# Three small edits: a square moved behind the residual, eight bias additions moved from ScalarE to VectorE, an activation table loaded earlier

## The chip, the cores and the metric

The kernel runs on one core of a Trainium2 chip. The metric is the time of one execution on the device in microseconds (us); the median of three executions of the kernel before is 2815.58 us, the lowest 2815.47 and the highest 2816.88.

TensorE is called PE in the profile, ScalarE ACT, VectorE DVE, GpSimd POOL, and SyncE SP.

## The reference

Two transformer stacks run one after the other on 256 tokens of width 1024, in fp32.

The first stack puts 16 meta tokens in front (272 rows) and has two layers. A layer is: a SwiGLU feed-forward and a layer norm; a mixer (short convolution and latent attention with gates) and a layer norm; a second feed-forward and a layer norm. In the latent attention the query latents (256 columns) and the key-value latents (128 columns) are each normalized by their root mean square before they are projected again:

```python
q = (rms_norm(c_q, q_norm_g) @ w_uq).reshape(...)
kv = (rms_norm(c_kv, kv_norm_g) @ w_ukv).reshape(...)
```

The second stack has two layers. Both start with an rms norm and a token mixer with three branches. The first layer then has a dense SwiGLU and the second a mixture of 8 experts (top 2 of a router, `swiglu` of width 3584 for each). A last rms norm closes the kernel:

```python
h = layer_norm(ALPHA * h + 0.5 * swiglu(h, ...), ln_g[l, 2], ln_b[l, 2])   # end of the first stack
...
h = rmsnorm(x, norm_g)                                                     # start of the second
...
gate = softmax(top_v); out = silu(xb @ w_gate[e]) * (xb @ w_up[e]) @ w_down[e]
```

## The kernel before, in words

Each engine has a program of its own, written out in full by hand; semaphores are the only link between them, and an engine runs its program strictly in order. Activations lie transposed: 8 chunks of 128 channels on the partitions, 272 or 256 tokens along the free dimension. Every fp32 product is made of three fp16 matmuls, high times high, high times low and low times high (`parts`, L2081 to L2085). Weights come in units of 2048 columns through four slots. For each unit SP starts the loads, ACT makes the high half (`split`, L705), DVE the low half (L1260), PE multiplies, and ACT or DVE takes the sums out of PSUM. PE may start a unit when its low half is there (`parts_ready`) and when the PSUM banks that it writes have been emptied (`act_evac`, `vec_evac`).

Three places matter here.

**Place A, the latents, in the loop over the six units of `win` (L900 to L919), once in each of the first stack's two layers.** ACT's program at step u=2 is: the square of the three latent chunks into `tmp` (L904); `residual` (L796 to L800), eight biased copies that turn the scaled rows `sq` into the residual `h`; the split of a later unit (L705); and the emptying of unit 2 (L898). PE, when it has finished unit 2, waits for `lat_squared` (L2334), sums the squares (L2335 to L2337), places the rotary key (L2340), and goes on with unit 3. ACT takes the square roots at step u=3 (L913, L914), DVE inverts them and scales the latents (L1461, L1464), and PE waits for the two halves of the result (`lat_ready`, L2344) after unit 5.

**Place B, the last layer norm of the first stack (`layer_norm` with `last=True`).** DVE scales chunk after chunk: `t(c)` (L1386) makes `sq[c]`, `u(c+1)` (L1376) centers the next chunk, and a drain ends the step. ACT follows each chunk with two operations: the square of `sq[c]` plus the bias (L788), which PE sums for the rms norm behind it (L2285), and the same sum unsquared, the residual `h[c]` (L789). After the eighth chunk PE runs its filler matmuls (`keep_warm`, L2237), ACT takes the root (L828) and DVE the reciprocal (L1404).

**Place C, the router of the second stack's second layer.** PE makes the router's logits and transposes the tokens into PSUM (L2698, two halves); DVE finds the two best experts. ACT's program here is: the exponential of the difference of the two (L1187); the high halves of the two token halves out of PSUM (L1190, `xt_hi_ready`); and then a one-element Silu (L1191) before which the table with Silu is loaded. DVE makes the low half of each token half behind ACT (`rows_low`, L1776), between the two the ranks (L1780) and the marks of the first expert (L1787). PE gathers the first expert's rows with them (L2742), ACT empties the gathered rows (L1199, L1231), and PE starts on the first expert's weights (L2083). The eight experts follow one another in the same program, with six slots of weights.

Of the kernel before, what the change touches and what calls it, by code (L numbers as in the profile page):

```python
# [39 lines left out]
META = 16  # L40
# [654 lines left out]
def act_program(act, k, i, out):  # L695
# [80 lines left out]
    def layer_norm(n, b0, q, following, last=False):  # L776

        act.wait_ge(k.ln_rest, n + 1)
        t = kept(n)
        act.activation(k.tmp[:, 1, t], k.ps[:, 4, t], ACT.Square).then_inc(k.rest_squared, 1)  # L780
        act.wait_ge(k.ln_spread, n + 1)
        act.activation(k.std[:, 0, t], k.tmp[:, 1, t], ACT.Sqrt, bias=k.eps[:, 0:1]).then_inc(k.ln_std, 1)
        split(following + 2, q, UNIT)
        if last:

            for c in range(KC):
                act.wait_ge(k.ln_scaled, n * KC + (c + 1))
                act.activation(k.sq2[:, c, :], k.sq[:, c, META:T1], ACT.Square, bias=k.col[:, b0 + c:b0 + c + 1]).then_inc(k.rms_squared, 1)  # L788
                act.activation(k.h[:, c, META:T1], k.sq[:, c, META:T1], ACT.Identity, bias=k.col[:, b0 + c:b0 + c + 1])  # L789
            return  # L790

        for c in range(KC):
            act.wait_ge(k.ln_scaled, n * KC + (c + 1))
            act.activation(k.x_hi[:, c, t], k.sq[:, c, t], ACT.Identity, bias=k.col[:, b0 + c:b0 + c + 1]).then_inc(k.x_hi_ready, 1)
# [80 lines left out]
    for l in range(DEPTH):  # L875
# [23 lines left out]
        win, mid, side = S1["win"], S1["mid"], S1["side"]  # L899
        for u in range(win.units):  # L900
            late = u + AHEAD - win.units
            if u == LAT_SQUARED:
                act.drain()
                act.activation(k.tmp[:, :, :], k.mix1[:, 12:15, :], ACT.Square).then_inc(k.lat_squared, 1)  # L904
            if u == 2:
                residual(C1["ln_b"], ALL1)
            if u >= 1:
                split(win.first + u + AHEAD, q, win.size if late < 0 else win.after[late])

            if u == LAT_ROOT:  # L910
                act.wait_ge(k.lat_mean, l + 1)
                act.drain()
                act.activation(k.std[:, 0, :], k.ps[:, 4, 0:T1], ACT.Sqrt, bias=k.eps[:, 1:2], scale=float(D) / 256)  # L913
                act.activation(k.std[:, 1, :], k.ps[:, 5, 0:T1], ACT.Sqrt, bias=k.eps[:, 1:2], scale=float(D) / 128).then_inc(k.lat_std, 1)  # L914
            if u == LAT_HI:
# [269 lines left out]
        expert_split(u, 0)  # L1185
    act.wait_ge(k.lg_ready, 1)
    act.activation(k.rt[:, :, 1], k.rt[:, :, 0], ACT.Exp).then_inc(k.lg_exped, 1)  # L1187
    for t in range(2):
        act.wait_ge(k.xt_turned, t + 1)
        act.activation(k.xt_hi[:, t, :], k.ps[:, 2 * t:2 * t + 2, :].rearrange("p b n -> p (b n)"), ACT.Copy).then_inc(k.xt_hi_ready, 1)  # L1190
    act.activation(k.warm[:, :], k.eps[:, 0:1], ACT.Silu)  # L1191

    def gathered(bank):
        return k.ps[:, bank:bank + 2, :].rearrange("p b (c s) -> p (b c) s", s=P)
# [60 lines left out]
def vec_program(vec, k, i, out):  # L1255
# [114 lines left out]
    def layer_norm(n, g0, b0, last=False):  # L1370
# [19 lines left out]

        def lo(c):
            return vec.scalar_tensor_tensor(k.x_lo[:, c, cols], k.sq[:, c, cols], k.col[:, b0 + c:b0 + c + 1], k.x_hi[:, c, cols], ALU.add, ALU.subtract)
        for c in range(KC + 1):
            if last:

                if c < KC:
                    t(c)
            else:
                scaled(c, t, lo, (n + 1) * KC)
            vec.drain()  # L1400
# [679 lines left out]
def pe_program(pe, k, i, out):  # L2080
# [240 lines left out]
    for l in range(DEPTH):  # L2321
# [8 lines left out]
        def towards_latents(u):  # L2330
# [1 line left out]
                return  # L2332

            pe.wait_ge(k.lat_squared, l + 1)  # L2334
            pe.matmul(k.ps[:, 4, 0:T1], k.mean_w[:, :], k.tmp[:, 0, :], start=True, stop=False)  # L2335
            pe.matmul(k.ps[:, 4, 0:T1], k.mean_w[:, :], k.tmp[:, 1, :], start=False, stop=True)
            pe.matmul(k.ps[:, 5, 0:T1], k.mean_w[:, :], k.tmp[:, 2, :], start=True, stop=True).then_inc(k.lat_mean, 1)  # L2337

            for n in range(2):
                a = pe.matmul(k.ps[0:QK, 6 + n, 0:T1], k.place[:, n, :], k.mix1[0:ROPE, 15, :], start=True, stop=True)  # L2340
# [584 lines left out]
```

## Time and profile before

| | before |
|---|---|
| median of 3 executions | 2815.58 us |
| the profiled execution | 2815.58 us |
| its span, first to last instruction | 2813.8 us |
| what lies around the span | 1.8 us |
| mean granted clock of TensorE | 0.992 |
| PE busy | 2750.0 us (98%) |
| DVE busy | 1981.1 us (70%) |
| ACT busy | 1612.1 us (57%) |
| POOL busy | 700.7 us (25%) |

The profiled execution took the median's time, so its span can be used with no correction. A busy PE includes matmuls that overlap in its pipeline, so 98% does not say that there is nothing to gain; what counts at each place is which wait ends last there. In a timeline the columns are the start, the duration, the engine, the source line, the operation and its tiles, how many, and in brackets how long the engine stood idle before it and what released it.

### The profile page before, as it was taken

What the parts mean: (1) busy time and instruction counts of PE and PEld (TensorE: products, weight loads), DVE (VectorE), ACT (ScalarE), POOL (GpSimd) and SP (SyncE); (2) the same over time, 40 slices, a digit from 0 to 9 for tenths busy, and PEclk for the clock granted to TensorE, in tenths of its full rate; (3) what the DMA queues carried; (4) which work ended last, traced back from release to release, by engine and by line L of the source; (5) the groups of instructions that cost most, each with busy time, mean ns of one, the idle gap of its engine ahead of it and who ended that gap; (6) DMA issues with size and microseconds to landing.
All of it is one profiled execution on the core that took longest, in us unless ns stands there. A gap on an engine that the chain in (4) does not pass through costs nothing.

```text
span 2813.8 us, 68029 instructions
## 1 busy us (share of the span) xinstructions
PE 2750.0 (98%) x28028; PEld 2294.9 (82%) x28028; DVE 1981.1 (70%) x1906; ACT 1612.1 (57%) x1731; POOL 700.7 (25%) x562
## 2 busy tenths in 40 slices
PE   9999999999999999999999999999999999999998
PEld 8887778888877888887788897888879788797794
DVE  4567575465575755666755566779899898998986
ACT  5445653353356544555544455656777776777765
POOL 4315022121122221120122002144234243242331
PEclk9999999999999999999999999999999999999999
DMA  9764367576643676553666663469999999999995
GB/s 240 172 198 130 92 181 201 164 192 175 188 138 109 177 209 174 162 187 109 179 182 171 205 196 125 150 229 369 377 394 380 386 388 377 394 382 384 389 378 228
DMA packets 657516, 665.64 MB, mean 237 GB/s; under 512 B 25302, under 2 KB 513116, under 8 KB 657276
## 3 DMA queue, kind: packets, MB, share of 16 engines
q1 hardware_dynamic: 655696, 659.75, 71.3%
q8 instruction: 189, 3.10, 0.5%
q0 software_dynamic: 704, 0.59, 0.4%
q10 hardware_dynamic: 876, 1.79, 0.2%
q14 instruction: 51, 0.42, 0.0%
HBM read 661.01 MB, written 1.05 MB: 235 GB/s over the span
## 4 chain that ended last, share of the span: by engine, by line
PE 90%; DVE 4%; ACT 2%; issue 2%; DVEq 2%; POOLq 0%; POOL 0%; ACTq 0%
PE ps L2083 23%; PE ps L2085 23%; PE ps L2084 23%; PE ps L2809 3%; PE ps L2808 3%; PE ps L2807 3%; PE ps L2124 1%; PE ps L2130 1%; PE ps L2125 1%; DVE w_lo L1260 1%; PE ps L2412 1%; PE ps L2432 1%; DVE sq L1386 1%; PE ps L2500 1%; PE ps L2502 1%
## 5 line engine op out<-in xcount | busy, mean ns | idle before, releaser
L2083 PE MATMUL ps<-x_hi,w_hi 128*128 128x128 f16 (+2 forms) x5440 | 1231.1, 250 | 15.1 <-DVE prod L1275 5.4
L2085 PE MATMUL ps<-x_hi,w_lo 128*128 128x128 f16 (+2 forms) x5440 | 1230.5, 250 | 0.0
L2084 PE MATMUL ps<-x_lo,w_hi 128*128 128x128 f16 (+2 forms) x5440 | 1230.5, 250 | 0.0
L1260 DVE SCALAR_TENSOR_TENSOR w_lo<-w,w_hi 128x2048 f16<-128x2048 f32 (+4 forms) x338 | 692.7, 2060 | 303.3 <-ACT w_hi L705 301.4
L705 ACT ACTIVATE w_hi<-w 128x2048 f16<-128x2048 f32 (+4 forms) x338 | 560.9, 1669 | 94.8 <-PE ps L2085 70.5
L2083 PEld LDWEIGHTS ps<-x_hi,w_hi 128*128 128x128 f16 x5440 | 534.3, 98 | 70.4 <-issue 14.4
L2084 PEld LDWEIGHTS ps<-x_lo,w_hi 128*128 128x128 f16 x5440 | 534.2, 98 | 46.1
L2085 PEld LDWEIGHTS ps<-x_hi,w_lo 128*128 128x128 f16 x5440 | 534.1, 98 | 42.9
L1753 DVE SCALAR_TENSOR_TENSOR w_lo<-w,w_hi 128x2048 f16<-128x2048 f32 x224 | 534.3, 2411 | 40.6 <-ACT w_hi L1180 40.4
L1180 ACT ACTIVATE w_hi<-w 128x2048 f16<-128x2048 f32 x224 | 416.9, 1901 | 28.6 <-DMA w<-in_moe_w_gate 11.6
L2065 POOL CAST ff<-pb 128x512 f16<-128x512 f32 x56 | 135.5, 2419 | 568.2 <-DVE pb L1845 568.2
L2083 PE MATMUL ps<-ff,w_hi 128*128 128x272 f16 (+1 forms) x880 | 243.4, 277 | 0.0
L2084 PE MATMUL ps<-ff,w_hi 128*128 128x272 f16 (+1 forms) x880 | 243.4, 277 | 0.0
L2085 PE MATMUL ps<-ff,w_lo 128*128 128x272 f16 (+1 forms) x880 | 243.4, 277 | 0.0
L1180 ACT ACTIVATE ff<-mix 128x2048 f16<-128x2048 f32 x112 | 211.5, 1903 | 16.9 <-DMA mix<-in_moe_w_down 15.3
L718 ACT ACTIVATE tmp<-ps 128x272 f32<-128x272 f32 (+1 forms) x110 | 43.0, 391 | 299.9 <-PE ps L2085 297.1
L2083 PE MATMUL ps<-x_hi,ff 128*128 128x128 f16 x1024 | 173.2, 219 | 0.0
L2084 PE MATMUL ps<-x_lo,ff 128*128 128x128 f16 x1024 | 173.2, 219 | 0.0
L2067 POOL TENSOR_TENSOR ff<-pb,ff 128x512 f16<-128x512 f32 x56 | 167.6, 2993 | 8.1 <-issue 0.2
L1902 POOL CAST ff<-prod 128x272 f32 (+3 forms) x110 | 57.6, 524 | 442.0 <-DVE prod L1275 441.5
L1275 DVE SCALAR_TENSOR_TENSOR prod<-tmp,ps 128x272 f32<-128x272 f32 (+1 forms) x110 | 47.4, 431 | 133.8 <-ACT tmp L718 123.9
L1753 DVE SCALAR_TENSOR_TENSOR mix<-mix,ff 128x2048 f16<-128x2048 f32 x56 | 130.9, 2337 | 14.7 <-ACT ff L1180 14.7
(390 smaller groups left out, 4307.5 us busy)
## 6 DMA issues: line engine op xcount, KB each, us to landing
w<-in_ffn_w_up SPq DMA_DIRECT2D x176, 512.0 KB, 5.0
w<-in_moe_w_gate SPq DMA_DIRECT2D x80, 1024.0 KB, 8.4
w<-in_moe_w_up SPq DMA_DIRECT2D x80, 1024.0 KB, 8.6
w<-in_moe_w_down SPq DMA_DIRECT2D x64, 1024.0 KB, 7.7
w<-in_w_in SPq DMA_DIRECT2D x112, 512.0 KB, 4.6
mix<-in_moe_w_down SPq DMA_DIRECT2D x48, 1024.0 KB, 8.1
w<-in_mix_w_in SPq DMA_DIRECT2D x64, 512.0 KB, 5.0
mix<-in_moe_w_gate SPq DMA_DIRECT2D x32, 1024.0 KB, 8.9
```

Of the source, the lines that this page charges most:

```text
L705: act.activation(k.w_hi[:, s, 0:size], k.w32[:, s, 0:size], ACT.Copy, scale=WS).then_inc(k.hi_ready, 1)
L1180: act.activation(k.e_hi[s], k.e_w32[s], ACT.Copy, scale=WS).then_inc(k.hi_ready, 1)
L1260: vec.scalar_tensor_tensor(k.w_lo[:, s, 0:size], k.w32[:, s, 0:size], WS, k.w_hi[:, s, 0:size], ALU.mult, ALU.subtract).then_inc(k.parts_r ...
L1753: vec.scalar_tensor_tensor(k.e_lo[s], k.e_w32[s], WS, k.e_hi[s], ALU.mult, ALU.subtract).then_inc(k.parts_ready, 1)
L2065: pool.tensor_copy(k.a_hi3[:, rows, :], prod)
L2067: pool.tensor_tensor(k.a_lo3[:, rows, :], prod, k.a_hi3[:, rows, :], ALU.subtract).then_inc(k.ff_ready, 1)
L2083: pe.matmul(acc, w_hi, x_hi, start=first, stop=False)
L2084: pe.matmul(acc, w_hi, x_lo, start=False, stop=False)
L2085: return pe.matmul(acc, w_lo, x_hi, start=False, stop=last)
L2807: pe.matmul(acc, k.a_hi3[:, ff, :], k.e_hi[s][:, w], start=ff == 0, stop=False)
L2808: pe.matmul(acc, k.a_lo3[:, ff, :], k.e_hi[s][:, w], start=False, stop=False)
L2809: a = pe.matmul(acc, k.a_hi3[:, ff, :], k.e_lo[s][:, w], start=False, stop=ff == EC - 1)
```

## The change

Three edits, in ACT's, DVE's and PE's programs. The arithmetic is the same.

1. Place A: at step u=2 the square of the latents goes from the front of the step to behind the residual and the split, just ahead of the emptying of unit 2. Its result goes to `sq[0:3]` instead of `tmp`, since the residual has by then read `sq`, and PE reads it there. The drain ahead of the roots at u=3 goes.
2. Place B: ACT's eight additions of the bias into `h` go (L789). DVE does them as `plain(c)`, one step behind the scaling: chunk c-1 in step c, behind `t(c)` and `u(c+1)` and ahead of the drain.
3. Place C: the one-element Silu, and so the load of its table, goes from behind the two copies of the tokens to directly behind the exponential.

```diff
@@ layer_norm, ACT @@
                 act.activation(k.sq2[:, c, :], k.sq[:, c, META:T1], ACT.Square, bias=...).then_inc(k.rms_squared, 1)
-                act.activation(k.h[:, c, META:T1], k.sq[:, c, META:T1], ACT.Identity, bias=...)
@@ the loop over win, ACT @@
-            if u == LAT_SQUARED:
-                act.drain()
-                act.activation(k.tmp[:, :, :], k.mix1[:, 12:15, :], ACT.Square).then_inc(k.lat_squared, 1)
             if u == 2:
                 residual(C1["ln_b"], ALL1)
             if u >= 1:
                 split(win.first + u + AHEAD, q, win.size if late < 0 else win.after[late])
+            if u == LAT_SQUARED:
+                act.drain()
+                act.activation(k.sq[:, 0:3, :], k.mix1[:, 12:15, :], ACT.Square).then_inc(k.lat_squared, 1)
             if u == LAT_ROOT:
                 act.wait_ge(k.lat_mean, l + 1)
-                act.drain()
                 act.activation(k.std[:, 0, :], k.ps[:, 4, 0:T1], ACT.Sqrt, ...)
@@ before the experts, ACT @@
     act.activation(k.rt[:, :, 1], k.rt[:, :, 0], ACT.Exp).then_inc(k.lg_exped, 1)
+    act.activation(k.warm[:, :], k.eps[:, 0:1], ACT.Silu)
     for t in range(2):
         act.wait_ge(k.xt_turned, t + 1)
         act.activation(k.xt_hi[:, t, :], ..., ACT.Copy).then_inc(k.xt_hi_ready, 1)
-    act.activation(k.warm[:, :], k.eps[:, 0:1], ACT.Silu)
@@ layer_norm, DVE @@
+        def plain(c):
+            vec.tensor_scalar(k.h[:, c, META:T1], k.sq[:, c, META:T1], k.col[:, b0 + c:b0 + c + 1], None, ALU.add)
         for c in range(KC + 1):
             if last:
                 if c < KC:
                     t(c)
+                if c > 0:
+                    plain(c - 1)
@@ towards_latents, PE: the three matmuls of L2335 to L2337 read k.sq[:, 0..2, :] instead of k.tmp[:, 0..2, :] @@
```

## Rows read from the trace of the kernel before

**Rows 1.** The page, part 4: the chain that ended last, by engine.

```profile
PE 90%; DVE 4%; ACT 2%; issue 2%; DVEq 2%; POOLq 0%; POOL 0%; ACTq 0%
```

**Rows 2.** Timeline of ACT in the experts: the emptying that ends each expert.

```profile
2108.68 1.11 ACT L1219 ACTIVATE mix<-ps,gate_now 128x1024 f16<-128x1024 f32 x1 [5.13 <-PE ps L2809]
...
2338.30 1.11 ACT L1219 ACTIVATE mix<-ps,gate_now 128x1024 f16<-128x1024 f32 x1 [4.38 <-PE ps L2809]
```

**Rows 3.** Timeline of ACT at place A, layer 0.

```profile
220.37 0.62 ACT L898 ACTIVATE mix<-ps 128x544 f32<-128x544 f32 x1
221.07 0.88 ACT L904 ACTIVATE tmp<-mix 128x816 f32<-128x816 f32 x1
221.87 3.39 ACT L799 ACTIVATE h<-sq,col 128x272 f32<-128x272 f32 x8
225.16 1.89 ACT L705 ACTIVATE w_hi<-w 128x2048 f16<-128x2048 f32 x1
226.96 0.60 ACT L898 ACTIVATE mix<-ps 128x544 f32<-128x544 f32 x1
```

**Rows 4.** Timeline of PE at place A, layer 0.

```profile
224.76 0.62 PE L2335 MATMUL ps<-tmp,mean_w 128*128 128x272 f32 x2
```

**Rows 5.** The square's line: count, duration in ns, first and last start.

```profile
L904 ACT ACTIVATE tmp<-mix x2: 883/884/884, 221.1 to 800.4; 128x816 f32<-128x816 f32 x2
```

**Rows 6.** Timeline of DVE: the latents' low half, for which PE waits after unit 5.

```profile
241.65 1.00 DVE L1476 TENSOR_TENSOR y_lo<-sq,y_hi 128x816 f16<-128x816 f32 x1
```

**Rows 7.** The chain that ended last, behind unit 5: start, duration, what.

```profile
244.06 0.13 PE ps L2085
...
244.73 1.90 ACT w_hi L705
```

**Rows 8.** Timeline at place B, one step of DVE and ACT behind it.

```profile
1155.90 0.48 DVE L1386 SCALAR_TENSOR_TENSOR sq<-h,col,rstd 128x256 f32<-128x256 f32 x1
1156.31 0.41 DVE L1376 TENSOR_TENSOR h<-h,ps 128x256 f32<-128x256 f32 x1
1156.42 0.51 ACT L788 ACTIVATE ff<-sq,col 128x256 f32<-128x256 f32 x1 [0.59 <-DVE sq L1386]
1156.80 0.48 DVE L1386 SCALAR_TENSOR_TENSOR sq<-h,col,rstd 128x256 f32<-128x256 f32 x1
...
1164.54 1.75 DVE L1404 RECIPROCAL rstd<-tmp 128x256 f32<-128x256 f32 x1 [1.91 <-ACT tmp L828]
```

**Rows 9.** Timeline of DVE: a tensor_scalar of 256 columns, then a drain.

```profile
1193.23 0.35 DVE L1561 TENSOR_SCALAR ff<-mix,col 128x256 f32<-128x256 f32 x1
1193.67 1.61 DVE L1564 SCALAR_TENSOR_TENSOR ff<-mix,col,ff 128x255 f32<-128x255 f32 x3
```

**Rows 10.** Timeline at place C.

```profile
1865.12 0.21 ACT L1187 ACTIVATE rt<-rt 128x2 f32<-128x2 f32 x1 [1.35 <-DVE rt L1765]
1865.23 1.00 ACT L1190 ACTIVATE mix<-ps 128x1024 f16<-128x1024 f32 x1
...
1866.27 1.23 DVE L1776 TENSOR_TENSOR mix<-ps,mix 128x1024 f16<-128x1024 f32 x1
...
1867.55 1.28 ACT L1191 ACT_TABLE_LOAD   x1
...
1868.84 0.20 ACT L1191 ACTIVATE warm<-eps 128x1 f32<-128x1 f32 x1
...
1869.43 1.02 ACT L1199 ACTIVATE x_hi<-ps 128x1024 f16<-128x1024 f32 x1 [0.39 <-PE ps L2742]
...
1872.34 0.26 PE L2083 MATMUL ps<-x_hi,w_hi 128*128 128x128 f16 x1 [1.20 <-ACT x_lo L1231]
```

**Rows 11.** Busy time by stretch (us; PE, PEld, DVE, ACT, POOL), granted clock, DMA share, GB/s.

```profile
1157.00:1164.00 7.00, 5.65 (x19) 2.79 (x20) 5.18 (x13) 6.61 (x16) 0.00 (x0) 1.00 0.01 2
...
1864.00:1872.30 8.30, 5.95 (x50) 5.15 (x48) 7.82 (x23) 5.78 (x8) 4.54 (x4) 0.71 0.39 128
1872.30:1880.00 7.70, 7.66 (x102) 7.69 (x103) 7.23 (x12) 3.52 (x3) 7.70 (x5) 0.72 0.81 278
```

More of the change, by code:

```diff
@@ L788, in layer_norm @@
                 act.activation(k.sq2[:, c, :], k.sq[:, c, META:T1], ACT.Square, bias=k.col[:, b0 + c:b0 + c + 1]).then_inc(k.rms_squared, 1)
-                act.activation(k.h[:, c, META:T1], k.sq[:, c, META:T1], ACT.Identity, bias=k.col[:, b0 + c:b0 + c + 1])
             return
@@ L2334, in towards_latents @@
             pe.wait_ge(k.lat_squared, l + 1)
-            pe.matmul(k.ps[:, 4, 0:T1], k.mean_w[:, :], k.tmp[:, 0, :], start=True, stop=False)
-            pe.matmul(k.ps[:, 4, 0:T1], k.mean_w[:, :], k.tmp[:, 1, :], start=False, stop=True)
-            pe.matmul(k.ps[:, 5, 0:T1], k.mean_w[:, :], k.tmp[:, 2, :], start=True, stop=True).then_inc(k.lat_mean, 1)
+            pe.matmul(k.ps[:, 4, 0:T1], k.mean_w[:, :], k.sq[:, 0, :], start=True, stop=False)
+            pe.matmul(k.ps[:, 4, 0:T1], k.mean_w[:, :], k.sq[:, 1, :], start=False, stop=True)
+            pe.matmul(k.ps[:, 5, 0:T1], k.mean_w[:, :], k.sq[:, 2, :], start=True, stop=True).then_inc(k.lat_mean, 1)
             for n in range(2):
```

## The prediction, made before the changed kernel was built or run

> **What bounds the kernel now.** I read the page first, its chain that ended last. TensorE holds 90% of it, DVE 4% and ACT 2% [rows 1]. So a change on another engine moves the time only where PE stands waiting for it, and the thing to look up at each place is who waits last. The second view is the timeline of the experts, which fill the last third. One ACT operation ends each expert; from its start at 2108.68 to that two experts later, 2338.30, there are 229.62 us, 114.81 for each, and PE releases it each time [rows 2]. A delay ahead of the experts therefore has nothing in them that could give it back. The other views are the timelines of the three edited places, where the reader should compare the end of one engine's operation with the start of the next engine's.
>
> **Place A, the square behind residual and split.** Before, ACT empties unit 1 (220.37 to 220.99), squares from 221.07 to 221.95, runs the eight residual copies from 221.87, the split from 225.16, and empties unit 2 from 226.96 [rows 3]. PE takes up the squares at 224.76, right behind unit 2, with no idle time before it [rows 4]. So the squares lie ready 2.81 us early, and PE pays nothing for them. After the edit the chain on ACT is: an operation that follows undrained starts 0.08 before its predecessor ends (221.87 against 221.95), so the residual starts at 220.99 - 0.08 = 220.91; the split follows 225.16 - 221.87 = 3.29 later, at 224.20, and lasts 1.89, to 226.09; the drain costs the 0.08 seen between 220.99 and 221.07, so the square runs from 226.17 to 227.05; the hand-over to the next engine costs 0.04, as between DVE's end at 1156.38 and ACT's start at 1156.42 [rows 8]. PE begins at 227.09 in place of 224.76: a stall of 2.33 us. The second layer has the same square at 800.4 [rows 5], so twice, 4.66 us.
>
> What is queued behind the late square: only the emptying of unit 2, and since the step's operations are the same ones in another order, it keeps its time of about 226.96. PE needs it for unit 4, over 5 us later. The split comes a microsecond earlier, but PE has not been waiting for it. The roots at step u=3 need PE's three sums. At 0.62 each [rows 4] these end at 227.09 + 3 x 0.62 = 228.95 at the latest; ACT gets to the roots at about 226.96 + 0.60 + 1.89 = 229.45 [rows 3], so they are not delayed, and the drain taken away ahead of them (0.08) lies in cover.
>
> Who gives the stall back? PE's next waits for others. The latents' low half ends at 242.65 [rows 6], while PE finishes unit 5 at 244.19, later anyway. Behind it the chain goes over ACT's split at 244.73 [rows 7], but in ACT's program that split stands behind the emptying of unit 5, so it starts from PE's own end and moves with it. I find no clock of another engine that would absorb the stall, and cost it in full: 4.66 us. Bounds: nothing, if a later wait absorbs it, and 4.66.
>
> **Place B, the bias additions on DVE.** DVE sets the pace: a step is t (0.48 us, next start 0.41 later) and u (0.41), and the next t starts 0.90 after the first [rows 8]. ACT's two operations fit into the same 0.90: its square starts 0.04 after DVE's scaling ends and never falls behind. Removing one of the two from ACT therefore gains nothing, least of all at the end: the last pair is followed by PE's sum and the root, which waits for PE.
>
> The added operation is a tensor_scalar of 128x256 in fp32 out of SBUF. The same form takes 0.35 us, and with a drain behind it the next operation starts 0.44 later [rows 9]. In a step it slips between u and the drain: t to u 0.41, u to plain 0.41 - 0.07 = 0.34 (0.07 being the overlap of t and u, 1156.38 - 1156.31), plain and drain 0.44. A step is 1.19 in place of 0.90, so 0.29 more. Steps 1 to 6 with plain(0) to plain(5) lie ahead of the last scaling: 6 x 0.29 = 1.74 us. plain(6) and plain(7) come behind it and hide: DVE sits idle for 1.91 us ahead of the reciprocal [rows 8], and the two need 2 x 0.44, about 0.9. Without that cover they would cost 0.9 more. Bounds: nothing, if ACT's additions had been what held the pace, and 8 x 0.44 = 3.5. I take 1.74, for the nearest row is the same operation of the same size.
>
> Here the trace and the skill differ. The row has 0.35 us for the tensor_scalar. The Trainium skill, page "VectorE: DVE Perf Modes", section "The TRN2 errata — SBUF-src ops pay a fixed extra latency per instruction", tables a VectorE operation out of SBUF at 58 cycles plus half the elements in a doubled mode, which for 256 elements is an estimate of 0.19 us; by it the step would grow by 0.13 and place B would cost 0.8. The row decides.
>
> **Place C, the table loaded before the copies.** Before, ACT takes the exponential at 1865.12, the first copy from 1865.23 to 1866.23, and DVE starts the low half at 1866.27, 0.04 later: it is gated by the copy. Load (1.28) and Silu (0.20) come at 1867.55, and are over at 1869.04, before ACT's next task at 1869.43, for which PE releases it [rows 10]. They cost nothing there. After the edit the load starts right behind the exponential, at about 1865.36, ends at 1866.64, and the Silu is over at 1866.85; the first copy starts 0.09 before that, 1866.76, and ends at 1867.76. DVE's low half starts at 1867.80, 1.53 later than before. Behind it on DVE wait the ranks and the first expert's marks, behind those PE's gather, ACT's emptying of it (1869.43), and PE's first expert matmul at 1872.34 [rows 10]: one chain, each link started by the one before, so 1.53 us later at its end. The second copy ends about 1868.7, before anything asks for it.
>
> The granted clock bears on this term. Its mean is 0.71 from 1864 to 1872.3, where PE is busy for 5.95 of 8.3 us, and 0.72 in the 7.7 us from the first expert matmul on [rows 11]. With the two levels 0.5 (1.2 GHz) and 1 (2.4 GHz) a mean of 0.72 is 7.7 x 0.28 / 0.5 = 4.3 us at the lower one. If the clock returns at the same moment, a later start wastes less: of the 1.53 us half comes back, 0.77 net. If the return moves with the work, all 1.53 stay. I take the middle, 1.15. Bounds: 1.53 - 2.15 = -0.6, if the first expert loses nothing to the clock, and 1.53 + 2.15 = 3.7, if it loses twice as much.
>
> The Trainium skill, page "ScalarE: Activation LUTs", section "What ACT_TABLE_LOAD costs", adds a drain of about 1.38 us to each load. No such gap stands in the trace, where the Silu follows the load at 1868.84, 0.01 after its end; by the page, place C would come out at an estimated 2.5 in place of 1.15.
>
> **Sum.** 4.66 + 1.74 + 1.15 = 7.55 us. The profiled execution took 2815.58, which is the median as well, so 2823.1 us, 0.27% more. About 0.2%, 5.6 us here, is what a measurement of this kernel can tell from no change.
>
> **The rivals.**
> *Absorbed at place A (not slower by a measurable amount).* PE would have waited behind unit 5 in any case, for the latents or for a load, and gives the two stalls back there. Price: 4.66 off, leaving 2.9, 2818.5 us. For it: PE's end at 244.19 is followed by ACT's split on the chain, so PE truly waits there. Against: that wait starts from PE's own unit [rows 7], and the latents are 1.5 us early [rows 6, 7]. It decides as soon as 1.9 of the 7.55 come back, less than one layer's stall.
> *The clock falls where it held.* At place B PE is busy 5.65 of 7 us and the clock holds at 1.00 [rows 11]; with steps a third longer PE thins out, and at place A it stands for 2.33 us. At place C the clock did fall once PE stood. A low stretch as long as the one at place C, 4.3 us, costs half of that, 2.15, for each place hit: 2825.3 with one.
> *ACT had been the brake at place B.* Its two operations nearly fill the step of 0.90; relieved of one, it would leave DVE's step alone to set the pace, and DVE's longer step then costs less than reckoned, about nothing: 2823.1 - 1.74 = 2821.4. Against: no wait of DVE on ACT in any step, and ACT starts 0.04 behind DVE [rows 8].
> *The low stretch at C is skipped.* The shift of all that lies ahead changes what PE does when the clock is next granted; with no low stretch C comes to -0.6, the lower bound above: 4.66 + 1.74 - 0.6 = 5.8, 2821.4.
> *The new operations cost other than their rows.* If the drain hid the end of DVE's addition as a following operation hides it, it would add 0.35 - 0.07 - 0.09 = 0.19 to a step (0.09 from 0.44 - 0.35, [rows 9]): 1.1 at place B, 2822.5; this is the side of the page on VectorE. If ACT stood behind the table load for another load's length, 1.28, place C would be so much dearer, 2824.4; this is the side of the page on ScalarE. The rows as they stand speak against both.
>
> **How the numbers follow.** Forecast as summed 0.54; absorbed 0.14; clock falls elsewhere 0.12; ACT the brake 0.04; low stretch skipped 0.06; the two new operations 0.04 and 0.03; 0.03 for what I do not see. The likeliest gives 2823.1. The low end of the range takes in the absorbed case, 2818.5; the high end is one low stretch more, 2825.3, and place B at its bound, 1.8 more: 2827.0. Slower by over 0.2% are the forecast, the falling clock, the two new operations and half of the two cases at 2821.4, whose 5.8 us is on the bound: 0.54 + 0.12 + 0.07 + 0.05 = 0.78, less 0.04 for the forecast's small margin, 0.74. Within 0.2%: absorbed 0.14, the other halves 0.05 and that margin 0.04, 0.23. Faster: 0.03, what I do not see, since all terms together would have to turn.
>
> **What the profile after would show.** Place A: in both layers PE idle for 2.3 us ahead of the sums of squares, released by ACT's square, and unit 3 later by as much. Place B: DVE's steps 1.19 apart, its reciprocal's idle time shrunk to about 1.0. Place C: the first copy at about 1866.8 plus the shift ahead of it, DVE's low half released by ACT, the first expert matmul 1.5 later against the exponential. The experts 114.81 apart as before. The prediction is wrong if PE's idle time behind unit 5 shrinks by what it gained ahead of unit 3, if DVE's steps do not lengthen, or if the granted clock has low stretches elsewhere.

## The result and the profile after

| | before | after |
|---|---|---|
| median of five executions each | 2815.58 us | 2831.99 us |
| lowest and highest | 2814.93 to 2816.98 us | 2827.72 to 2833.26 us |
| ratio after to before, as recorded | | 1.0053, 95% interval 1.0042 to 1.0065 |
| span of the profiled execution | 2813.8 us | 2828.8 us |
| mean granted clock | 0.992 | 0.989 |
| predicted | | 2823.1 us, range 2818.5 to 2827.0 |

The changed kernel is slower, as predicted, but by 16.4 us in place of 7.5, and outside the range. The 15.0 us between the two profiled spans are what this section takes apart. One execution of the kernel before, beside the runs e5 to e8 below, took 3446.52 us at a granted clock of 0.807 and is in none of the comparisons.

The page's first part and the chain by engine, after:

```profile
PE 2757.3 (97%) x28028; PEld 2297.7 (81%) x28028; DVE 1984.5 (70%) x1914; ACT 1608.3 (57%) x1723; POOL 702.2 (25%) x562
...
PE 91%; DVE 4%; ACT 2%; issue 2%; DVEq 1%; POOLq 0%; ACTq 0%; POOL 0%
```

The instruction counts show the edit: eight operations fewer on ACT, eight more on DVE, 28028 on PE in both. But PE is busy for 7.3 us longer than before (2750.0) with the same instructions. A stall would show as idle time, not as busy time; at a lower clock the same matmuls last longer: the 32 that gather the rows at place C take 2.81 us before, in a stretch with a mean granted clock of 0.70, and 3.60 after, at 0.50. The chain has hardly changed from [rows 1], and says nothing of the loss.

**Place A.** Timeline of ACT and of PE, first layer (before: [rows 3, 4]), and of PE in the second:

```profile
221.04 0.61 ACT L897 ACTIVATE mix<-ps 128x544 f32<-128x544 f32 x1
221.54 3.40 ACT L798 ACTIVATE h<-sq,col 128x272 f32<-128x272 f32 x8
224.84 1.90 ACT L705 ACTIVATE w_hi<-w 128x2048 f16<-128x2048 f32 x1
226.82 0.88 ACT L908 ACTIVATE sq<-mix 128x816 f32<-128x816 f32 x1
227.62 0.60 ACT L897 ACTIVATE mix<-ps 128x544 f32<-128x544 f32 x1
```

```profile
227.76 0.72 PE L2336 MATMUL ps<-sq,mean_w 128*128 128x272 f32 x2 [2.17 <-ACT sq L908]
...
810.85 0.73 PE L2336 MATMUL ps<-sq,mean_w 128*128 128x272 f32 x2 [2.17 <-ACT sq L908]
```

The square stands behind residual and split, and PE is idle for 2.17 us until it. The whole program lay 0.66 us late before place A (221.04 against 220.37 for the emptying of unit 1). With that, PE takes up the squares at 227.76 in place of 224.76, so 2.34 us later than it would have. The first two sums behind the idle time take 0.72 us where they took 0.62, and the emptying of unit 3 comes at 236.19 where it came at 233.09: this layer adds 2.44. The other adds 2.44 as well (812.40 to 819.27, after a lag of 4.43).

The 0.66 us were there before anything that was edited. They come from the 60 matmuls of constants that open the program on PE, before and after:

```profile
1.36 9.18 PE L2313 MATMUL ps<-mean_w 128*128 128x128 f32 x60 [1.36 <-DVE eps L1434]
```

```profile
1.36 9.86 PE L2314 MATMUL ps<-mean_w 128*128 128x128 f32 x60 [1.36 <-DVE eps L1435]
```

The same 60 matmuls took 9.77 us in the profile of e5_after_again and 8.39 in that of e3_c_only, so this differs from one execution to the next.

**Place B.** Timeline of DVE, two steps of the last norm, and its reciprocal (before: [rows 8]):

```profile
1165.87 0.48 DVE L1384 SCALAR_TENSOR_TENSOR sq<-h,col,rstd 128x256 f32<-128x256 f32 x1
1166.28 0.41 DVE L1374 TENSOR_TENSOR h<-h,ps 128x256 f32<-128x256 f32 x1
1166.61 0.35 DVE L1392 TENSOR_SCALAR h<-sq,col 128x256 f32<-128x256 f32 x1
1167.03 0.48 DVE L1384 SCALAR_TENSOR_TENSOR sq<-h,col,rstd 128x256 f32<-128x256 f32 x1
...
1174.04 1.75 DVE L1405 RECIPROCAL rstd<-tmp 128x256 f32<-128x256 f32 x1 [1.21 <-ACT tmp L827]
```

A step is 1.16 us (1165.87 to 1167.03) against 0.90, and the reciprocal's idle time has shrunk from 1.91 to 1.21: the last two additions hide there.

**Place C.** Timeline of ACT and of DVE (before: [rows 10]):

```profile
1879.52 0.21 ACT L1185 ACTIVATE rt<-rt 128x2 f32<-128x2 f32 x1 [1.35 <-DVE rt L1766]
1879.74 1.28 ACT L1186 ACT_TABLE_LOAD   x1
1881.04 0.20 ACT L1186 ACTIVATE warm<-eps 128x1 f32<-128x1 f32 x1
1881.15 1.92 ACT L1189 ACTIVATE mix<-ps 128x1024 f16<-128x1024 f32 x2
1886.16 1.02 ACT L1197 ACTIVATE x_hi<-ps 128x1024 f16<-128x1024 f32 x1 [3.10 <-PE ps L2743]
```

```profile
1882.19 1.23 DVE L1777 TENSOR_TENSOR mix<-ps,mix 128x1024 f16<-128x1024 f32 x1 [1.48 <-ACT mix L1189]
```

From the exponential's start to DVE's low half there are 2.67 us (1879.52 to 1882.19), before 1.15 (1865.12 to 1866.27): 1.52 more, and DVE waits 1.48 of it. Behind that the delay grows, for PE's gather runs at the lower level (the 3.60 us above in place of 2.81). The first expert matmul comes at 1889.04 in place of 1872.34, against the exponential 2.30 us later. Then most of it comes back, because the first expert now has the full clock, where it had 0.72 [rows 11]:

```profile
1889.04 0.22 PE L2084 MATMUL ps<-x_hi,w_hi 128*128 128x128 f16 x1 [1.21 <-ACT x_lo L1229]
```

```profile
1888.90:1896.60 7.70, 7.56 (x136) 7.59 (x137) 6.94 (x12) 5.51 (x4) 7.70 (x5) 1.00 0.88 297
```

At the first emptying inside the experts (1894.68 against 1879.97) 0.31 us of the 2.30 is left.

**The clock.** Stretches of both kernels at the attention stage of the first layer, and after at two later places. The columns are as in [rows 11]; the one behind POOL's count is the granted clock. Before:

```profile
336.00:340.00 4.00, 4.00 (x22) 2.61 (x22) 1.23 (x1) 1.69 (x4) 0.00 (x0) 0.64 0.51 148
340.00:344.00 4.00, 4.00 (x30) 2.86 (x28) 0.44 (x1) 0.88 (x2) 0.00 (x0) 0.93 0.40 116
344.00:348.00 4.00, 4.00 (x37) 3.37 (x35) 0.75 (x1) 2.28 (x3) 0.00 (x0) 1.00 0.02 4
...
1786.00:1798.00 12.00, 12.00 (x103) 9.97 (x102) 11.83 (x12) 7.20 (x9) 0.00 (x0) 1.00 0.29 86
1844.00:1852.00 8.00, 7.96 (x73) 7.16 (x74) 2.62 (x6) 2.03 (x6) 3.34 (x5) 1.00 1.05 396
```

After:

```profile
336.00:340.00 4.00, 1.78 (x7) 0.90 (x7) 2.36 (x6) 3.24 (x9) 0.00 (x0) 0.82 0.15 41
340.00:344.00 4.00, 4.00 (x21) 2.62 (x20) 1.23 (x1) 0.81 (x3) 0.00 (x0) 0.50 0.58 172
344.00:348.00 4.00, 4.00 (x27) 2.69 (x26) 0.30 (x1) 0.88 (x2) 0.00 (x0) 0.83 0.17 51
...
1786.00:1798.00 12.00, 9.78 (x68) 7.62 (x66) 7.55 (x8) 10.25 (x14) 0.00 (x0) 0.86 0.44 130
1844.00:1852.00 8.00, 6.09 (x41) 4.79 (x42) 5.15 (x8) 5.12 (x5) 1.83 (x2) 0.79 0.01 2
```

In the first group the missing clock before is (4 x 0.36 + 4 x 0.07) / 0.5 = 3.4 us at the lower level (1.2 GHz); after, (4 x 0.18 + 4 x 0.50 + 4 x 0.17) / 0.5 = 6.8 us. Read in this way over the whole span, but for the last 11 us or so, where PE runs out of work, before has 37.5 us at the lower level and after 54.6. The low stretches stand at the same kinds of place in both: the attention stages, the wo and wout stages behind them, the end of the second stack. What differs is which of them are there, and whether one is single, double or triple.

Nearly every event stands in both traces, so its lag can be followed:

| stretch of the program | lag grows by | to | what it is |
|---|---|---|---|
| opening matmuls | 0.66 | 0.66 | before anything that was edited |
| place A, layer 0 | 2.44 | 3.10 | own stall |
| attention, layer 0 | 1.33 | 4.43 | 6.8 us low in place of 3.4 |
| place A, layer 1 | 2.44 | 6.87 | own stall |
| attention, layer 1 | 1.04 | 7.91 | 6.8 in place of 3.4 |
| place B | 1.60 | 9.51 | own stall |
| second stack, attention, layer 0 | 1.59 | 11.10 | 6.8 in place of 3.4 |
| its wout stage | -1.61 | 9.49 | 3.4 before, none after |
| attention, layer 1 | 1.72 | 11.21 | 6.8 in place of 3.4 |
| near 1792 and near 1847 | 3.18 | 14.39 | 3.4 twice, none before |
| place C, into the first expert | 0.32 | 14.71 | 2.30 late, of which the clock gave back 2.0 |
| experts to the end | 0.3 | 15.0 | |

Own stalls: 2.44 + 2.44 + 1.60 + 0.32 = 6.8 us. Clock at places nobody edited: 1.33 + 1.04 + 1.59 - 1.61 + 1.72 + 3.18 = 7.25 us, for 54.6 - 37.5 = 17.1 us more at the lower level, 0.42 us for each. That account is of two executions. The trace of e5_after_again, the changed kernel once more, has the same low stretches, 54.6 us of them. But a single trace can't say that the change brought them: e14_shift_11 below is the kernel before up to place B, and in its trace, too, the low stretch at the attention stage of layer 0 is 6.8 us long, and the lag grows by 1.4 us there. Before, and in e14_shift_11:

```profile
335.00:345.00 10.00, 9.33 (x61) 6.50 (x60) 2.11 (x3) 3.57 (x10) 0.00 (x0) 0.83 0.36 106
```

```profile
335.00:345.00 10.00, 9.33 (x47) 5.92 (x47) 1.85 (x4) 3.72 (x10) 0.00 (x0) 0.66 0.36 106
```

So the low stretches of one kernel differ between executions, and whether the clock's share is the change's doing or chance is what the means of many runs had to tell.

### The profile page after: what moved, and what is told of

The parts are those of the page before. It is cut to its first block, busy times and chain, and to the rows that moved or that the text cites. A ratio compares the mean times of both kernels' runs of the same rounds, so it can differ in the third digit from the quotient of the medians.

```text
span 2828.8 us, 68027 instructions
## 1 busy us (share of the span) xinstructions
PE 2757.3 (97%) x28028; PEld 2297.7 (81%) x28028; DVE 1984.5 (70%) x1914; ACT 1608.3 (57%) x1723; POOL 702.2 (25%) x562
## 4 chain that ended last, share of the span: by engine, by line
PE 91%; DVE 4%; ACT 2%; issue 2%; DVEq 1%; POOLq 0%; ACTq 0%; POOL 0%
PE ps L2084 23%; PE ps L2086 23%; PE ps L2085 23%; PE ps L2808 3%; PE ps L2809 3%; PE ps L2810 3%; PE ps L2125 1%; PE ps L2131 1%; PE ps L2126 1%; PE ps L2433 1%; PE ps L2413 1%; DVE w_lo L1258 1%; PE ps L2743 1%; PE ps L2502 1%; PE ps L2501 1%
## 5 line engine op out<-in xcount | busy, mean ns | idle before, releaser
L1952 POOL TENSOR_TENSOR x_lo<-sq,x_hi 128x256 f16<-128x256 f32 (+1 forms) x32 | 40.0, 1249 | 410.6 <-ACT sq L843 410.6
```

## The experiments

Each was run 5 to 12 times beside 27 to 30 executions of the kernel before on its chip; the mean difference below is over these executions, with its standard error. The clock is the mean of the executions' granted clocks, 0.9922 for the kernel before over 114 executions. Over all 270 executions a straight line with one offset for each kernel gives 2.2 us for each 0.001 of mean clock. Since 0.001 of 2814 us is 5.6 us at the lower level, that is 0.40 us for each, as in the table above. "Own" is the offset, the difference that is left at equal clock.

| run | median us | ratio, 95% | mean difference | clock | own |
|---|---|---|---|---|---|
| e1_a_only | 2822.76 | 1.0029 (1.0016 to 1.0042) | +8.0 ± 1.3 | 0.9907 | +4.5 |
| e2_b_only | 2818.29 | 1.0019 (1.0009 to 1.0030) | +5.0 ± 1.2 | 0.9900 | 0.0 |
| e3_c_only | 2815.08 | 1.0006 (0.9996 to 1.0015) | +0.4 ± 0.6 | 0.9925 | +1.0 |
| e4_filler_10 | 2818.49 | 1.0015 (1.0005 to 1.0024) | +4.4 ± 1.1 | 0.9920 | +3.9 |
| e5_after_again | 2832.12 | 1.0060 (1.0048 to 1.0073) | +16.8 ± 0.5 | 0.9882 | +8.1 |
| e6_a_fill | 2820.24 | 1.0017 (1.0008 to 1.0026) | +5.1 ± 0.6 | 0.9918 | +4.6 |
| e7_b_fill | 2820.00 | 1.0018 (1.0009 to 1.0027) | +5.0 ± 0.8 | 0.9902 | +0.8 |
| e8_wo_fill | 2813.36 | 0.9997 (0.9988 to 1.0007) | -0.6 ± 1.2 | 0.9918 | -1.3 |
| e9_b_warm | 2818.23 | 1.0018 (1.0008 to 1.0027) | +5.4 ± 1.2 | 0.9905 | +1.4 |
| e10_b_shift | 2823.52 | 1.0025 (1.0014 to 1.0035) | +8.0 ± 1.4 | 0.9904 | +3.7 |
| e11_after_fill | 2827.96 | 1.0042 (1.0029 to 1.0055) | +13.5 ± 0.8 | 0.9898 | +7.8 |
| e12_more_fill | 2812.15 | 0.9992 (0.9981 to 1.0002) | -1.6 ± 1.3 | 0.9934 | +0.8 |
| e13_shift_3 | 2817.21 | 1.0005 (0.9996 to 1.0014) | +1.4 ± 0.8 | 0.9917 | +0.3 |
| e14_shift_11 | 2817.39 | 1.0010 (1.0001 to 1.0019) | +2.6 ± 0.6 | 0.9919 | +1.9 |
| e15_shift_15 | 2818.02 | 1.0010 (1.0001 to 1.0019) | +2.9 ± 0.8 | 0.9924 | +3.2 |
| e16_after_all_fill | 2826.57 | 1.0037 (1.0023 to 1.0051) | +9.3 ± 1.8 | 0.9910 | +6.6 |

The own column is good to 1.5 or 2 us, no better. Part B's trace has a stall of 1.6 where it says 0.0. By the table above a low stretch of 3.4 us costs from 1.0 to 1.7 us by its place, and one slope cannot know which of them a kernel has.

**The three parts, each alone.** e1_a_only is the diff's edits at place A, e2_b_only those at place B, e3_c_only the one at place C.

> Edit A alone (square behind residual and split). The changed kernel's trace has 2.44 us of stall at each of the two places A, and low-clock stretches in the two attention stages behind them that are 6.8 us long where the kernel before has 3.4. Theory 1 (own stalls only, the sum of the prediction): 4.9 us slower than before. Theory 2 (a delay also moves the work against the moments at which the clock is granted, and lengthens low stretches by about 1.5 us of lost work each): 4.9 plus 1.0 to 1.5 for each attention stage hit, about 7 to 8 us by the end of the first stack, and more or less later, low stretches listed in its trace. Rival 3 (the whole 15 us belongs to edit A): 15 us slower.

> Edit B alone (eight additions on VectorE). Own cost by its trace in the changed kernel: six steps longer by 0.266 us, 1.6 us. Theory 1: 1.6 us slower. Theory 2: 1.6 plus or minus whole low-clock stretches behind it, 1 to 1.7 us each, and nothing changed ahead of it. Rival: over 5 us, if the operation hurts something not yet seen.

> Edit C alone (table load ahead of the copies). Theory 1 and the prediction: the low half on VectorE starts 1.53 us later; 0.8 to 1.5 us slower in all. Theory 2: the same, since nothing but the experts comes behind it, with at most one low stretch of difference right there (1.7 us).

A alone costs 8.0 and B alone 5.0, where their stalls are 4.9 and 1.6; the clock of both is lower. C alone costs nothing that can be told from zero. So neither A nor B is its own stall and no more. In the trace of A alone the clock falls at place A itself. Its stretches around the idle time:

```profile
224.00:226.00 2.00, 0.85 (x8) 0.49 (x5) 0.00 (x0) 2.00 (x2) 0.00 (x0) 1.00 0.54 180
226.00:228.00 2.00, 0.98 (x4) 0.78 (x4) 1.97 (x1) 1.92 (x3) 0.00 (x0) 0.90 0.00 0
228.00:230.00 2.00, 2.00 (x5) 1.05 (x4) 1.01 (x2) 1.68 (x3) 0.00 (x0) 0.50 0.26 41
230.00:232.00 2.00, 2.00 (x7) 0.86 (x6) 2.00 (x2) 0.47 (x2) 0.00 (x0) 0.50 0.99 326
```

PE stood for 2.17 us, and is at 0.5 right after. In the changed kernel's trace the same idle time has no low stretch behind it, and of six such idle times in three traces (two layers each in e1_a_only, after and e5_after_again) this is the only one that has.

**A delay in which PE is busy.** e4_filler_10 is the kernel before with ten small matmuls of constants ahead of the wait for the squares:

```diff
+            for _ in range((10, 10)[l]):
+                pe.matmul(k.ps[:, 7, 0:P], k.mean_w[:, :], k.mean_w[:, :], start=True, stop=True)
             pe.wait_ge(k.lat_squared, l + 1)
```

> The kernel before with ten filler matmuls (128x128 fp32 into a bank that nothing else uses then) on TensorE at both places A, ahead of the sums of squares: a delay of about 2.4 us each with TensorE busy, nothing reordered. Theory 1: 2 x 2.4 = 4.7 us slower. Theory 2 (only the shift in time counts): the same low stretches of 6.8 us in the attention stages as with edit A, 7 us or more slower. Rival 4 (the idle time at place A or the new order is what lengthens the low stretches): the low stretches stay 3.4 us long, 4.7 us slower, and less than edit A alone.

The same delay, made by work, costs 4.4 and leaves the mean clock where it was. Its profile would say otherwise: it fell on the slowest of the ten executions, 2827.49 us, with 54.6 us at the lower level and 6.8 in both attention stages of the first stack. The other nine lie between 2816.68 and 2819.54.

**Part A with PE kept busy, and the whole change again.** e6_a_fill is part A with the same ten matmuls; PE now works where it stood, and the square comes as late as ever. e5_after_again is the changed kernel once more.

> Part A alone, and ten small matmuls of constants (some 0.235 us each) on TensorE ahead of its wait for the latent squares, in both layers, so that TensorE isn't idle there; the squares come as late as with part A alone. Idle theory (the idle 2.17 us at place A is itself what lowers the clock, there in the profile of part A alone at 227.5 to 234.5, and perhaps what carries on to the attention stage): the mean difference falls from +7.9 (part A alone) to +4.3 to +5.3, with no low stretch near 227. Shift theory (a delay of 2.4 us per layer moves the attention stage against the clock, whatever TensorE did meanwhile): as part A alone, +7 to +9. Rival: the fillers run past the arrival of the squares and cost up to 0.5 us per layer.

> The changed kernel unchanged, beside the kernel before on one chip, in the same rounds as the three below. Own stalls plus clock (the theory now): the stalls of the parts add up (place A +4.9, place B +1.6, place C +1.5, together +8.0), and the rest of the +16 is time that TensorE spends at the granted clock of 0.5 further on; so mean granted clock again below that of before by 0.003 to 0.004, and +14 to +17 in all. Chance alone (the low stretches fall differently in each execution and the +16 was bad luck): +8 to +10 and the clock within 0.001 of before.

The whole change is again at +16.8, with a narrow spread (2830.09 to 2832.67) and the lowest clock of all: the +16 is systematic. Filled, A costs 5.1 ± 0.6 in place of 8.0 ± 1.3, near the clock of the kernel before; by itself that gain is only twice its error, and the pair below has to bear it out. The same stretches of e6_a_fill:

```profile
224.00:226.00 2.00, 2.00 (x20) 1.93 (x18) 0.10 (x1) 1.91 (x3) 0.00 (x0) 1.00 0.52 173
226.00:228.00 2.00, 2.00 (x14) 1.72 (x13) 2.00 (x1) 2.00 (x3) 0.00 (x0) 1.00 0.00 0
228.00:230.00 2.00, 2.00 (x11) 1.06 (x10) 1.01 (x2) 1.90 (x3) 0.00 (x0) 1.00 0.29 29
```

**The same cure in the changed kernel.** e11_after_fill has ten matmuls at place A; e16_after_all_fill also has nine ahead of each wo stage, seven ahead of each wout stage and five behind the rank sums (L2704).

> The changed kernel, and ten small matmuls of constants on TensorE ahead of its wait for the latent squares in both layers. Own stalls are those of the changed kernel (+8.0 to +8.5). If TensorE's idle at place A is what took the clock down there and in the attention stage, as parts A alone (+7.8) and A with the fillers (+5.1) say, the clock part falls from 8.5 to 5.5 or less: +11 to +14 against +16.8. If the clock part of the whole change comes from the delays only: +16 to +17.

> The changed kernel with all the fillers so far: ten ahead of the wait for the latent squares, nine and seven ahead of the wo and wout stages, five behind the rank sums. The own stalls stay (+8); with only place A filled it was +13.5 at a clock of 0.9898. If TensorE's idle ahead of dense work is what the clock answers to: clock at 0.9915 or more, +7 to +10. If the delays alone decide: clock 0.9895 to 0.990, +12 to +14.

+16.8 falls to +13.5 and to +9.3 (its five executions spread from 2818.83 to 2827.22, so that figure is loose), the clock rises from 0.9882 to 0.9898 and 0.9910, and the own time stays within its uncertainty: 8.1, 7.8, 6.6. The loss beyond the stalls is clock, and part of it can be had back by giving PE something to do. At place A that is 3.3 ± 1.0 us. The rest of the fall to +9.3 is not all the change's loss: the fillers of the later stages make the kernel before faster too, by 1.6 ± 1.3 (e12_more_fill below), and against that kernel e16_after_all_fill is at 10.9 ± 2.2.

**Part B: is it thin work?** At place B PE waits in each step. e9_b_warm is part B with two matmuls behind each of its sums but the last; e7_b_fill has them in the later rms norms.

```diff
         a = rms_sum(k.sq2[:, c, :], first=c == 0, last=c == KC - 1)
+        if c < KC - 1:
+            for _ in range(2):
+                pe.matmul(k.ps[:, 7, 0:P], k.mean_w[:, :], k.mean_w[:, :], start=True, stop=True)
```

> Part B alone, and two small matmuls of constants (0.235 us each) on TensorE behind each sum of place B itself but the last, so that TensorE is busy there in the waits for the squares. Part B alone ran at a mean granted clock of 0.9900 against 0.9922 and cost +4.9, of which only some 1.6 is its own stall. Thin-work theory (TensorE's waits of 0.9 us per step at place B carry over into the second stack's clock): clock back to 0.9915 to 0.9925 and +1.3 to +2.3. Shift theory (what comes after is merely 1.6 us later): clock 0.990 as before, +4 to +5.5. Rival: the fillers hold up the sums, which would add up to 1.5 to either.

> Part B alone, and two small matmuls of constants (0.235 us each) on TensorE behind each chunk's sum of the rms norm but the last, in every rms norm of the second stack (the one at place B in the code of the first stack has its own loop and is left as it is). It tells little of place B itself, but whether a denser TensorE in these norms changes the low stretches of the second stack: if thin work there lowers the clock, mean difference below part B alone (+4.9), down to +1.6; if the fillers delay the sums, above it by up to 0.3 us for each norm; if neither, +4 to +5.

Neither helps: +5.4 and +5.0 against +5.0, at the same low clock. Thin work at place B is not shown to be it; e7_b_fill, whose fillers stand in later norms, says little of place B itself.

**A mere delay at place B.** e10_b_shift, e13_shift_3, e14_shift_11 and e15_shift_15 are the kernel before, with 7, 3, 11 and 15 matmuls of constants ahead of the last sum:

```diff
     for c in range(KC):
         pe.wait_ge(k.rms_squared, c + 1)
+        if c == KC - 1:
+            for _ in range(7):
+                pe.matmul(k.ps[:, 7, 0:P], k.mean_w[:, :], k.mean_w[:, :], start=True, stop=True)
         a = rms_sum(k.sq2[:, c, :], first=c == 0, last=c == KC - 1)
```

> The kernel before, and seven small matmuls of constants (1.65 us together) on TensorE ahead of the last sum at place B: the second stack starts as much later as with part B, and TensorE doesn't wait for it. Shift theory: mean clock 0.990, +4 to +5.5 as with part B. Thin-work theory: clock as before (0.992), +1.5 to +1.9.

> The kernel before, and three small matmuls of constants (0.7 us) on TensorE ahead of the last sum at place B. Seven of them (1.65 us) made the second stack start 1.65 us later and the whole 8 us longer on average, with the clock at 0.9904 instead of 0.9923. If the clock answers to where the work falls in time and not to how late it is: any mean clock between 0.990 and 0.994 and no order by size; time = 0.7 + 2.2 us for each 0.001 of clock lost. If it answers to the size of the delay: clock some 0.0008 down, +2 to +4.

> The same with eleven (2.6 us). Where the work falls: mean clock anywhere from 0.990 to 0.994, +2.6 and 2.2 us for each 0.001. By size of the delay: clock below 0.9904, +9 or more.

> The same with fifteen (3.5 us, about as long as one low stretch in the traces). Where the work falls: mean clock anywhere from 0.990 to 0.994, and if the place in time counts modulo the length of a stretch, then as the kernel before, 0.992 and +3.5. By size of the delay: clock at or below 0.990, +10 or more.

| delay put in | mean difference | clock |
|---|---|---|
| 0.7 us | +1.4 ± 0.8 | 0.9917 |
| 1.65 us | +8.0 ± 1.4 | 0.9904 |
| 2.6 us | +2.6 ± 0.6 | 0.9919 |
| 3.5 us | +2.9 ± 0.8 | 0.9924 |

There is no order by size: a delay of 1.65 us costs 8, one of 3.5 us costs 2.9. Three of the four cost their own length within the error, so the reading rests on the one of 1.65. What supports it is part B: e2_b_only, e7_b_fill and e9_b_warm also start the second stack some 1.6 us late, and they too have a clock of 0.9900 to 0.9905 and cost 5.0 to 5.4. One trace of each, which may be of an unlucky and a lucky execution, shows what a higher and a lower clock look like. The root behind the sum is late by the delay and no more, in e10_b_shift and in e15_shift_15 (1163.96 before, with the lag ahead of it at 0.2 us or less):

```profile
1165.82 0.47 ACT L828 ACTIVATE tmp<-ps,eps 128x256 f32<-128x256 f32 x1 [1.96 <-PE ps L2285]
```

```profile
1167.41 0.47 ACT L828 ACTIVATE tmp<-ps,eps 128x256 f32<-128x256 f32 x1 [3.74 <-PE ps L2285]
```

Then the attention stages of the second stack and its end, e10_b_shift:

```profile
1258.00:1268.00 10.00, 9.67 (x51) 6.18 (x50) 5.45 (x14) 7.29 (x15) 9.51 (x15) 0.66 0.54 178
1696.00:1704.00 8.00, 7.75 (x36) 4.87 (x37) 4.02 (x9) 5.36 (x11) 7.58 (x12) 0.57 0.42 130
1864.00:1886.00 22.00, 19.82 (x171) 19.33 (x170) 20.03 (x42) 14.07 (x12) 12.17 (x8) 0.61 0.51 177
```

and e15_shift_15:

```profile
1258.00:1268.00 10.00, 9.67 (x60) 6.44 (x60) 5.89 (x15) 7.13 (x15) 9.51 (x16) 0.83 0.41 123
1696.00:1704.00 8.00, 7.67 (x45) 4.94 (x43) 5.17 (x12) 5.29 (x11) 7.65 (x12) 0.79 0.41 132
1864.00:1886.00 22.00, 19.61 (x224) 18.81 (x224) 19.05 (x39) 15.06 (x14) 14.76 (x12) 0.77 0.57 191
```

With PE as busy in both, the first has about twice the missing clock: 0.34 against 0.17 in the first row, 0.43 against 0.21 in the second. From the root on, the lag of e15_shift_15 stays at 3.5 us up to the experts; that of e10_b_shift grows from 1.9 to 7.1.

**The cure in the kernel before.** Its own trace has a low stretch behind PE's idle times ahead of the wo stage of layer 0 (2.59 us) and of the first wout stage (2.16 us). e8_wo_fill puts nine and seven matmuls ahead of these stages, e12_more_fill five more behind the rank sums.

```diff
     def wo_norm(n, q, vec0, chunk):
         phase, t = S1["wo"], kept(n)
+        for _ in range(9):
+            pe.matmul(k.ps[:, 7, 0:P], k.mean_w[:, :], k.mean_w[:, :], start=True, stop=True)
         opening(phase, q, k.vec_evac, vec0, k.x_hi, k.x_lo, t, chunk, P, 256, True)
```

> The kernel before, and nine small matmuls of constants on TensorE (2.1 us) ahead of its wait for the first weights of each wo stage, seven (1.6 us) ahead of that of each wout stage, where the kernel before is idle 2.59 and 2.16 us and its clock falls to 0.5 right after for 3.4 us. Idle theory: the low stretches at 371 and 1398 are gone, each gives back 1.4 to 1.7 us, so 2812 to 2814 against 2815 to 2816, clock up by 0.001 or more. If the low stretches come from elsewhere and only happen to fall there: no change within 1 us. Rival: the fillers hold up the stage where the weights come earlier in an execution (wo in layer 1): up to +2.

> The kernel before with the fillers of the wo and wout stages (their run: own time -1.2 at equal clock, mean clock 0.9918 as before, runs between 2810 and 2820), and five more fillers (1.17 us) behind the rank sums, where TensorE waits 1.12 us in the low stretches of the end of the second stack. If the idle there has a part in the low stretches between 1862 and 1877: mean clock up to 0.993 or more, mean 2810 to 2813. If not: as the wo and wout fillers alone, mean 2813 to 2815.

The stretches at the wo stage of layer 0, before and in e8_wo_fill:

```profile
370.00:372.00 2.00, 1.49 (x10) 1.16 (x11) 0.86 (x3) 1.02 (x3) 0.28 (x2) 0.82 0.97 253
372.00:374.00 2.00, 2.00 (x11) 1.35 (x9) 0.44 (x1) 2.00 (x2) 0.51 (x1) 0.50 1.14 318
```

```profile
370.00:372.00 2.00, 1.41 (x13) 1.10 (x12) 1.33 (x4) 0.46 (x2) 0.65 (x1) 1.00 1.10 260
372.00:374.00 2.00, 2.00 (x20) 1.69 (x18) 0.00 (x0) 2.00 (x2) 0.70 (x1) 1.00 1.06 306
```

The stretch is gone and the program has gained 1.5 us behind it (ACT's next split at 381.76 in place of 382.87, with a lag of 0.38 ahead of it), and gains 1.66 more at the wout stage. But the gain is given back: in its trace there are longer low stretches in two attention stages (6.8 us in place of 3.4) and at the end of the stack (17 us in place of 10) and one more near 1778, against four that are gone, 41.0 us in place of 37.5 in all, and its mean is -0.6 ± 1.2. Whether the fillers moved them there or the execution drew them, one trace can't tell. The fullest version has the highest clock and the lowest mean of all, 0.9934 and -1.6 ± 1.3; its ratio's interval still reaches 1. I have no version that is shown to beat the kernel before.

## Why the prediction was wrong, point by point

- **Place A** was right in mechanism and in size: with the 0.66 us by which the program lay late, PE took up the squares 2.34 us later, against 2.33, and the layer lost 2.44, the other 0.10 being the slower first sums. The emptying of unit 2 kept its time, as I had it (227.62 is 226.96 and the 0.66). The stall was absorbed nowhere, so the rival of that name fell.
- **Place B** was right: a step 0.26 longer against 0.29, together 1.60 against 1.74, with the last two additions hidden. ACT was not the brake. The addition took 347 to 354 ns over its eight instances, the row's 0.35. The Trainium skill's figure, page "VectorE: DVE Perf Modes", section "The TRN2 errata — SBUF-src ops pay a fixed extra latency per instruction", would make it an estimated 0.19, and the trace disagrees with it.
- **Place C** delayed DVE by 1.52 us, 1.53 as worked out, and the table load brought no gap of its own: the Silu starts 0.02 behind the load's end (1881.02 to 1881.04). The drain that the Trainium skill adds, page "ScalarE: Activation LUTs", section "What ACT_TABLE_LOAD costs", is not in this trace either. But the first expert matmul came 2.30 us later against the exponential, not 1.5, since the gather ran at 0.50; and the first expert lost nothing to the clock, which gave 2.0 back. The net of 0.32, and +0.4 ± 0.6 for the part alone, lie inside my bounds of -0.6 to 3.7. But in it the slow gather (0.8), which I had not reckoned, is set against a clock that gave back more than the 0.4 I took, and that it comes out small is luck.
- **The step that failed is the sum.** It took what lies between the edited places to keep its time, and so put the clock there at nothing; in the traces that term is 7.25 us, and over the executions of e5_after_again 16.8 less 8.1, some 8.7. I had the right rival, "the clock falls where it held", gave it 0.12, let it act at the edited places alone, and priced it at one stretch of 2.15 us. Half of the measured difference is clock. A part of it hangs on PE's idle time at place A (8.0 against 5.1 filled, 16.8 against 13.5). The rest appears at stages that the change does not touch and merely shifts; for part B a delay of its size alone, with PE busy, cost at least as much. Why a shift changes the clock there is not shown. It should have been a term of the sum with a range, not a rival. The profile had given its scale: the kernel before has 37.5 us at the lower level, at 0.4 us each an estimated 15 us that are not fixed.
- **A reading behind that rival** was half right: "at place C the clock did fall once PE stood". The second low stretch there, from 1869.7, does stand behind PE's idle time of 1.12 us ahead of the gather. The first began at 1862.9, when PE had been busy for 6.98 of the last 7 us, so PE's idle time could not be the whole condition:

```profile
1856.00:1863.00 7.00, 6.98 (x61) 6.76 (x60) 6.02 (x10) 6.59 (x6) 0.00 (x0) 0.99 0.70 262
```

- **The range** failed for the same reason. Executions of the kernel before alone go from 2809.2 us at a clock of 0.995 to 2821.8 at 0.989, a width that three executions did not show.
- What I had written down as a sign of error, "if the granted clock has low stretches elsewhere", is what the trace showed.

What stays open: the parts alone add up to 8.0 + 5.0 + 0.4 = 13.4 ± 1.9 and the whole to 16.8 ± 0.5, and no run tells whether the difference is real. Why part B alone sits at a low clock in all its executions, and the delay of 1.65 us only in most of them, was not found. Which low stretches a given delay will bring I can't say ahead; the sweep shows only that the delay's size does not order them.

## What to carry to other kernels

Read the granted clock along the span before pricing an edit, and add up the time at the lower level: that sum, times the 0.4 us that each of its microseconds costs here, is the most that a change could win back, and it gives the scale of what a shift may lose beside its own stall (17.1 us more here, on 37.5). Take several executions of one kernel before reading a low stretch as the work of an edit. A stall in which TensorE stood cost more than its length here, and cheap matmuls of constants in front of the wait took some 3 us of that surcharge away. And before a 0.2% gain or loss is put down to an edit, try a plain delay of the same size in the same place: here it moved the time as much as the edit did.

## What the runs showed of the hardware that was not expected

- What a delay costs is not ordered by its length: 0.7, 1.65, 2.6 and 3.5 us at one place cost 1.4, 8.0, 2.6 and 2.9.
- The clock fell at 1862.9 in the trace of before although PE had been busy for 6.98 of the 7 us ahead.
- The low stretches in these traces come in pieces of 3.4 us or small multiples of it (3.4, 6.8, 10.2, up to 17 in e8_wo_fill). One piece costs 1.0 to 1.3 us in the first stack's attention stages and 1.6 to 1.7 in dense work and in the second stack. The Trainium skill, page "TensorE: Matmul & The Clock Gate", section "What's actually happening", says that the chip's watch over TensorE's activity runs freely and does not start with the kernel, so that the moment of a change of clock depends on where the work lands. The page gives it for the rise at a kernel's start, and there the traces agree: the same 60 opening matmuls took from 8.39 us (e3_c_only) to 9.86 (after). That it is also why low stretches in the middle of the kernel differ between executions, and answer to a shift, fits the traces and is not shown.
- An idle time of 2.17 us was followed by a low stretch once (part A alone, layer 0) and five times by none (its layer 1, and both layers of after and e5_after_again).
